# Prompt attention of a hybrid decoder: selected scores of unit n issued in turn with the sliding scores of unit n-1

## The reference

```python
p_c = masked_softmax(einsum('bqghd,bcgd->bqghc', qg, kc), mask_c)   # 63 compressed blocks
p_s = masked_softmax(einsum('bqghd,bqgmd->bqghm', qg, k_s), mask_s) # selected blocks, causal
p_w = masked_softmax(einsum('bqghd,bkgd->bqghk', qg, kw), mask_w)   # window of 512, causal
o = gt[..., 0:1] * o_c + gt[..., 1:2] * o_s + gt[..., 2:3] * o_w    # each o_x = p_x @ v_x
```

## Time and profile before

| | us |
|---|---|
| time, median of 2 runs | 3040.44 (3039.64 to 3041.25) |
| span of the profiled execution | 3041.8 |
| the four passes over the units, together | 472.50 |
| PE busy within them | 433.91 |

### The profile page before, as it was taken

One profiled execution on the slowest core, in us unless ns is written; L12 is line 12 of the kernel. 1 busy time (PEld: TensorE's weight loads), 2 busy tenths in 40 slices (PEclk: granted clock), 3 DMA queues, 4 the chain that ended last, 5 costly groups with the idle time before them and its releaser, 6 DMA issues. The chain is left out here.

```text
span 3041.8 us, 36642 instructions
## 1 busy us (share of the span) xinstructions
PE 2667.2 (88%) x12861; PEld 1881.7 (62%) x12861; DVE 1261.2 (41%) x2782; ACT 654.2 (22%) x1434; POOL 221.5 (7%) x197
## 2 busy tenths in 40 slices
PE   4989989898989877798989899599488889999999
PEld 2676867677676757465767666466255556666643
DVE  3456474756556465105453636345523330001012
ACT  2222121312222221003333334222032220000000
POOL 0012020101011020000000000022011100000000
PEclk8999999999999989897979697799688889999999
DMA  3101010110101000310000000354243314121001
GB/s 99 41 2 44 0 43 8 36 33 10 43 1 43 1 16 9 111 45 15 1 14 0 14 0 0 82 190 173 98 154 124 124 62 132 24 48 30 18 28 66
DMA packets 124355, 150.69 MB, mean 50 GB/s; under 512 B 30144, under 2 KB 107968, under 8 KB 115712
## 3 DMA queue, kind: packets, MB, share of 16 engines
q1 hardware_dynamic: 113152, 77.71, 9.4%
q0 software_dynamic: 11136, 72.17, 6.4%
HBM read 137.76 MB, written 16.26 MB: 51 GB/s over the span
## 5 line engine op out<-in xcount | busy, mean ns | idle before, releaser
L731 PE MATMUL g_ps<-hT,g_W 128*128 128x352 f32 x1536 | 487.4, 467 | 12.0 <-DMA g_W<-in_w_in_dram 12.0
L731 PEld LDWEIGHTS g_ps<-hT,g_W 128*128 128x128 f32 x1536 | 286.6, 194 | 151.1 <-issue 19.8
L2398 DVE SCALAR_TENSOR_TENSOR m_sg<-m_sg,m_ps 128x352 f32<-128x352 f32 x48 | 25.0, 521 | 360.6 <-PE m_ps L2338 360.6
L1369 PE MATMUL p_ps<-p_PTr,KV 128*128 128x128 f32 x1056 | 161.6, 305 | 1.9 <-ACT p_PTr L1428 1.9
L1369 PEld LDWEIGHTS p_ps<-p_PTr,KV 128*128 128x128 f32 x1056 | 143.4, 212 | 8.6 <-ACT p_PTr L1428 3.8
L1428 ACT COPY p_PTr<-p_ps 128x512 f32<-128x512 f32 (+3 forms) x176 | 86.2, 520 | 203.2 <-PE p_ps L1358 202.9
L2350 PE MATMUL m_ps<-m_Wo,m_mixed 128*128 128x512 f32 (+1 forms) x288 | 124.0, 593 | 1.4 <-DVE m_mixed L2401 1.4
L2331 PE MATMUL m_ps<-hT,Wgates 128*128 128x352 f32 x384 | 117.4, 465 | 1.5 <-DVEq L2387 1.5
L1389 PE MATMUL p_ps<-hT,Wpair 128*128 128x352 f32 x384 | 116.4, 466 | 1.2 <-SPq L1321 1.2
L1358 PE MATMUL p_ps<-identity,p_Pr 128*128 128x128 f32 x592 | 98.2, 302 | 20.2 <-DVEq L1501 20.0
L2331 PE MATMUL m_ps<-hT,m_Wgates 128*128 128x352 f32 x384 | 115.6, 459 | 0.0
(11 more groups left out here) (391 smaller groups left out, 4388.1 us busy)
## 6 DMA issues: line engine op xcount, KB each, us to landing
g_W<-in_w_in_dram SPq DMA_DIRECT2D x32, 512.0 KB, 5.2
n_x<-in_x_prompt_dram SPq DMA_DIRECT2D x8, 512.0 KB, 8.5
g_S<-in_state_gdn_dram SPq DMA_DIRECT2D x8, 512.0 KB, 7.0
out_dram<-g_S POOLq DMA_DIRECT2D x8, 512.0 KB, 3.9
Wpair<-in_w_in_dram SPq DMA_DIRECT2D x16, 256.0 KB, 4.4
Wgates<-in_w_in_dram SPq DMA_DIRECT2D x8, 512.0 KB, 5.2
m_Wgates<-in_w_in_dram SPq DMA_DIRECT2D x8, 512.0 KB, 4.8
m_Wo<-in_w_out_dram SPq DMA_DIRECT2D x1, 4096.0 KB, 16.2
```

The source lines that it names most:

```text
L731: ins = pe.matmul(ps[:, k.bank, 0:w], W[:, c_, kt, :], hT[:, kt, t0:t0 + w], start=kt == 0, stop=kt == KT - 1)
L1369: ins = pe.matmul(ps[:, k.bank, 0:P], v, PTr[0:r, u % 3, q, :], start=at + q == 0, stop=kind == "cmp")
```

## The change

Scores move into one function. In step n it waits for `slc_exp` of n-1 and `win_exp` of n-2, then issues the first slc part of unit n, the first win part of unit n-1, the second slc part, the second win part, and the cmp scores of n-1. Unit n and n-1 are of different groups, so the two use opposite 64 rows. Transposes and values follow for unit n-3, all in one piece. ACT's step is `exp_slc(n)`, the first two evacuations of n-3, `exp_win(n-1)`, the rest. DVE's step is the slc maximum of n, the win maxima of n-1, `weigh(n-2)`, `output(n-4)`. There are four `Pr` buffers for three, and three slots of `nmx` and `rs` for two. The loops run one step further.

```diff
-        Pr = [sb(f"Pr{n}", [P, CC + P]) for n in range(3)]
+        NPR = 4
+        Pr = [sb(f"Pr{n}", [P, CC + P]) for n in range(NPR)]
-        nmx = sb("nmx", [P, 2, 3])
-        rs = sb("rs", [P, 2, 3])
+        nmx = sb("nmx", [P, 3, 3])
+        rs = sb("rs", [P, 3, 3])
...
+                slc, win = [], []
+                if n < NU:
+                    pe.wait_ge(slc_exp, nth(i, n))
+                    slc = list(range(0, (units[n][0] + 1) * P, 512))
+                if 1 <= n <= NU:
+                    pe.wait_ge(win_exp, nth(i, n - 1))
+                    qt = units[n - 1][0]
+                    win = list(range(max(0, qt - 4) * P, (qt + 1) * P, 512))
+                for x in range(2):
+                    if x < len(slc):
+                        slc_part(slc[x])
+                    if x < len(win):
+                        win_part(win[x])
+                if win:
+                    cmp_part()
...
-                for n in range(NU + 2):
-                    if n < NU:
-                        scores_slc(i, n)
-                    if n >= 2:
-                        for u, _, ts in groups_of(units[n - 2][0])[:2]:
-                            turn(i, n - 2, u, ts)
-                    if n < NU:
-                        scores_win(i, n)
-                    if n >= 2:
-                        outputs(i, n - 2)
+                for n in range(NU + 3):
+                    scores(i, n)
+                    if n >= 3:
+                        for u, _, ts in groups_of(units[n - 3][0])[:2]:
+                            turn(i, n - 3, u, ts)
+                        outputs(i, n - 3)
...
-                for n in range(NU + 2):
-                    gs = groups_of(units[n - 2][0]) if n >= 2 else []
-                    for x in gs[:2]:
-                        evac(i, n - 2, *x)
-                    if n < NU:
-                        exp_slc(i, n)
-                    for x in gs[2:3]:
-                        evac(i, n - 2, *x)
-                    if n < NU:
-                        exp_win(i, n)
-                    for x in gs[3:]:
-                        evac(i, n - 2, *x)
+                for n in range(NU + 3):
+                    gs = groups_of(units[n - 3][0]) if n >= 3 else []
+                    if n < NU:
+                        exp_slc(i, n)
+                    for x in gs[:2]:
+                        evac(i, n - 3, *x)
+                    if 1 <= n <= NU:
+                        exp_win(i, n - 1)
+                    for x in gs[2:]:
+                        evac(i, n - 3, *x)
...
-                for n in range(NU + 3):
+                for n in range(NU + 4):
                     if n < NU:
-                        maxima(i, n, step)
+                        maxima_slc(i, n, step)
                     if 1 <= n <= NU:
-                        weigh(i, n - 1, step)
-                    if n >= 3:
-                        output(i, n - 3)
+                        maxima_win(i, n - 1, step)
+                    if 2 <= n <= NU + 1:
+                        weigh(i, n - 2, step)
+                    if n >= 4:
+                        output(i, n - 4)
```

More of the change, by code:

```diff
@@ L1327, in _, with scores, part, slc_part @@
         def _(pe):
[L1328 to L1334, removed]
+            def scores(i, n):
+                def part(n):
+                    qt, gr = units[n]
+                    rows = slice(gr * DN, (gr + 1) * DN)
+                    return qt, rows, qT[rows, qt * P:(qt + 1) * P]
+                def slc_part(k0):
+                    qt, rows, q = part(n)
@@ L1335, in scores_slc @@
                     w = min(512, (qt + 1) * P - k0)
                     ins = pe.matmul(s_slc[:, k0:k0 + w], q, g.slcT[rows, k0:k0 + w], start=True, stop=True)
[L1337 to L1345, removed]
+                    if k0 + w == (qt + 1) * P:
+                        ins.then_inc(slc_scores, 1)
@@ L1346, in scores_win, with win_part, cmp_part @@
+                def win_part(k0):
+                    qt, rows, q = part(n - 1)
+                    w0 = max(0, qt - 4) * P
                     w = min(512, (qt + 1) * P - k0)
                     pe.matmul(s_win[:, k0 - w0:k0 - w0 + w], q, g.winT[rows, k0:k0 + w], start=True, stop=True)
-                pe.matmul(s_win[:, 640:640 + NCB], q, g.kcT[rows, :], start=True, stop=True).then_inc(win_scores, 1)
+                def cmp_part():
+                    qt, rows, q = part(n - 1)
+                    pe.matmul(s_win[:, 640:640 + NCB], q, g.kcT[rows, :], start=True, stop=True).then_inc(win_scores, 1)
@@ L1357, in turn @@
                     c0 = {"slc": t * P, "win": WC + (t - max(0, qt - 4)) * P, "cmp": CC}[kind]
-                    ins = pe.transpose(ps[:, k.bank, q * P:(q + 1) * P], Pr[n % 3][:, c0:c0 + P], g.ident)
+                    ins = pe.transpose(ps[:, k.bank, q * P:(q + 1) * P], Pr[n % NPR][:, c0:c0 + P], g.ident)
                 ins.then_inc(a_filled, 1)
@@ L1410, in exp_slc @@
                 qt, gr = units[n]
-                w, m = (qt + 1) * P, n % 2
+                w, m = (qt + 1) * P, n % 3
                 act.wait_ge(slc_max, nth(i, n))
-                act.activation(Pr[n % 3][:, 0:w], s_slc[:, 0:w], ACT.Exp, bias=nmx[:, m, 0:1], accum_out=rs[:, m, 0:1]
+                act.activation(Pr[n % NPR][:, 0:w], s_slc[:, 0:w], ACT.Exp, bias=nmx[:, m, 0:1], accum_out=rs[:, m, 0:1]
                                ).then_inc(slc_exp, 1)
@@ L1417, in exp_win @@
                 qt, gr = units[n]
-                ww, m, out = (min(qt, 4) + 1) * P, n % 2, Pr[n % 3]
+                ww, m, out = (min(qt, 4) + 1) * P, n % 3, Pr[n % NPR]
                 act.wait_ge(win_max, nth(i, n))
@@ L1433, in _ @@
                     if x == "z":
-                        act.wait_ge(turn_done, i + 3)
+                        act.wait_ge(turn_done, i + NPR)
                     for s, (t0, w) in enumerate(THIRDS):
@@ L1459, in _, with maxima_slc @@
             v.wait_ge(c_loaded, 16)
-            for n in range(3):
+            for n in range(NPR):
                 v.memset(Pr[n][:, CC:CC + P], 0.0).then_inc(turn_done, 1)
-            def maxima(i, n, step):
+            def maxima_slc(i, n, step):
                 qt, gr = units[n]
-                m = n % 2
-                w, ww = (qt + 1) * P, (min(qt, 4) + 1) * P
+                m = n % 3
+                w = (qt + 1) * P
                 v.wait_ge(slc_scores, nth(i, n))
@@ L1469, in maxima, with maxima_win @@
                 v.tensor_reduce(nmx[:, m, 0:1], s_slc[:, 0:w], AX, ALU.max, negate=True).then_inc(slc_max, 1)
+            def maxima_win(i, n, step):
+                qt, gr = units[n]
+                m, ww = n % 3, (min(qt, 4) + 1) * P
                 v.wait_ge(win_scores, nth(i, n))
@@ L1485, in weigh @@
                 qt, gr = units[n]
-                m, pr = n % 2, Pr[n % 3]
+                m, pr = n % 3, Pr[n % NPR]
                 w, ww = (qt + 1) * P, (min(qt, 4) + 1) * P
```

## The result

The changed kernel takes 3063.91 us (median of two runs, 3058.96 and 3068.87) against 3040.44: a ratio of 1.007 (95% interval 1.0054 to 1.0087). It is a little slower, by less than 2%. Four later runs of the same kernel gave 3057.74 (3057.35 to 3061.16), ratio 1.0052 (1.0036 to 1.0067).

The account below looks back on a forecast made before the run. PE's own work was taken to set the step in the middle of a pass. -0.6 - 5.6 + 5.8 = -0.4 us a pass; 3041.8 - 1.6 + 9.6 (clock) gave 3050, own range 3020 to 3080.

Parts of the forecast that it names:

- the likeliest case: Whole kernel: forecast 3050 us, own range 3020 to 3080, chance 0.66.
- Overlap: Slc and win scores on opposite halves fully overlap; PE alone would be 12.6 us shorter in steps 8 to 15.
- The new wait: Values wait for copies behind exp_slc(n) on ACT; steps 8 to 14 come to 49.4 us against 50.00.
- First stretch: Steps 0 to 7 of a pass: 42.0 us against 47.60, a gain of 5.6 us.
- Drain: Step 15 and three draining steps of a pass: 25.9 us against 20.10, 5.8 us lost.
- Clock: PE's new gaps lower the clock: two falls a pass at 1.2 us each, 9.6 us in four passes.
- The rule on PSUM evacuation: Tiling speeds up TensorE but not evacuation, which may then bind; the saving doesn't come and time stays where it was.
- PE still sets the step: Rival: PE's work counts, about 20 us less a pass, 2960, halfway 3000; chance 0.12 with halfway cases.
- The halves don't overlap: Rival: slc's second part waits for a win matmul, 12 us a pass more, 3098; chance 0.12.
- The gaps cost the clock: Rival: lower clock in most steps from 8 on, 12 to 43 us a pass, 3090 to 3210; chance 0.10.

Follow-up runs that it names:

- on one half: Changed kernel with win and cmp scores of unit n-1 computed from unit n's 64 rows, so no overlap: 3113.64 us, ratio 1.0229.
- the reordered kernel: Changed kernel with the first two evacuations ahead of exp_slc(n) and the third ahead of exp_win(n-1): 2981.43 us, ratio 0.9802; second chip 2979.45.
- the kernel with the wait filled: Changed kernel plus 8 to 18 unread identity transposes in PE's wait in each of steps 8 to 15: 3045.72 us, ratio 1.0008.
- The reordered kernels: Changed kernel with two evacuations ahead of exp_slc(n): 3007.06 us; with the third also ahead of exp_win(n-1): 2981.43 us.

## Why the prediction was right, and where its terms were off

Direction and mechanism hold, and the time lies within the likeliest case's own range; the point was 8 to 14 us too low, and that it came so close is in part luck: two errors of opposite sign nearly cancelled. By its steps:

- *Overlap.* Taken as full, and it is: a win part costs 0.86 us on one half and nothing beside slc on the other. PE's busy time of the middle fell by 6.4 us (48.26 to 41.84), though that includes three stretches in which matmuls ran at half speed. In the reordered kernel, without such stretches, it is 38.61: 9.7 less in seven steps, where 12.6 in eight had been worked out. Starts within 0.02 us, which the prediction named as the sign, were not seen for the 512-column passes of step 14: they start some 0.2 us apart and interleave.
- *The new wait.* Values idle 1.24 to 2.34 us in steps 8 to 15 of pair 1, released by ACT's copy; 1.5 to 2.5 was said. The chain's sum for steps 8 to 14, 49.4 us, is for the full clock, and at the full clock it measures 50.2 (the kernel with the wait filled). Sums from rows of the old trace were good to 2%.
- *First stretch.* 38.6 us instead of 42.0. The lower clock lasted 27.3 us, until 31 us into the pass, where the sum put all steps up to 7 at that price; in the kernel before it lasted 41.0 us, and on one half 41.0 again. How much of the further gain is the overlap's own and how much comes from the earlier rise of the clock was not taken apart.
- *Drain.* 28.0 instead of 25.9. Step 15 was put at 8.8 and measures 8.8 with the wait filled, 10.4 with the fall; the step after it takes 6.6 rather than 6.1, the two last 5.5 each as said.
- *Clock.* This term was mis-sized. Two falls a pass at 1.2 us were taken; four came. The three in the middle cost 4.8 us together (55.0 less 50.2), the one in step 15 1.6, so 6.4 us a pass and not 2.4. Over four passes that is 16 us more than the forecast had.
- *Together.* Taking pair 1 for each of the four passes: +16 for the falls, +3.2 for the chain (0.8 a pass), +2 for the drain (0.5 a pass), -13.6 for the first stretch (3.4 a pass), 7.6 us above the forecast. The four passes measure 486.60 against 480.5 forecast (472.50 - 1.6 + 9.6), 6.1 above. The two-run median lies 14 us above the forecast, the four later runs 8. The two errors that nearly cancelled are the falls (+16) and the first stretch (-13.6).

The rule on PSUM evacuation that the prediction weighed (the Trainium skill, TensorEngine Tiling (Array Packing), Performance Considerations, PSUM Bottleneck) gives the outcome of the change as it stands: the saving did not come, and the wait is for the copies. The reordered kernels show that this was not the evacuation's capacity. With the same number of copies on the same engine the wait falls from 84.2 to 20.9 us when they stand ahead of the exps.

The rivals: *PE still sets the step* had its condition (under 0.5 us of wait a step) unmet at 1.3 us a unit; it is what happens in the reordered kernel, at 0.33 us and 2980 us, near the 2960 worked out for it. *The halves don't overlap* was priced at 48 us more and measured 50 to 56 when made true; it is not what happened. *The gaps cost the clock* was right in kind, with a granted clock of 0.91 rather than below 0.8.

Open: which wait drops the clock. In pair 1 falls followed waits of 1.86, 2.21, 2.34 and 2.33 us, but none followed waits of 1.73, 1.68 and 2.10. Busy time by stretch, as around the wait of 2.34 us above: here the wait of 2.10 us lies in the first row, and the dense work behind it, still at 1.00, in the second.

```profile
1606.00:1609.60 3.60, 1.52 (x15) 1.17 (x11) 2.88 (x7) 1.61 (x4) 0.00 (x0) 1.00 0.00 0
1609.70:1613.00 3.30, 3.30 (x29) 3.18 (x31) 2.28 (x9) 1.93 (x5) 0.00 (x0) 1.00 0.00 0
```

The length of the wait alone does not sort the cases (1.86 us did it, 2.10 did not), and no run tested what does. In the reordered kernels, where the values wait for 1.1 us at most, no fall came from step 8 on.

## What to carry to other kernels

When two matmul streams are packed side by side, look at once for the first thing behind them in the lists of the engines that drain PSUM: an operation that waits for the newest scores must not stand ahead of copies of older results, since PE then waits for copies that could have been made earlier. Here the packed scores were worth 72 us, and the place of the evacuations in ACT's list decided whether the kernel became 0.5 to 0.7% slower or some 2% faster. Price a new wait on PE twice: for its own length, and for the stretch at the lower clock that dense work behind it may run into (1.6 us here for a wait of some 2 us).

## What the runs showed of the hardware

- Matmuls on opposite 64 rows start out of their order in the program. `slc_part` is issued as a whole ahead of `win_part`, yet in the timeline of step 14 win's first pass (1612.76) starts before slc's first (1613.08), and win's second (1613.30) before slc's second (1613.51). The Trainium skill, TensorE: Matmul & The Clock Gate, Part 3, has matmuls in program order in start and end; the recorded starts differ from that for f32 passes on different rows.
- Two streams of 512 columns in f32, on 64 rows each, run at full rate: slc passes 0.43 us apart with or without win beside them.
- The clock fell after waits of about 2 us with dense work behind them; the earlier trace rows had shown a fall only in a stretch of 3.50 us without a matmul.
- With 112 more transposes in a pass, PE idled 2.6 to 3.0 us with "issue" as the cause ahead of each next pass (8.3 us in three), and the queue of instructions moved 60 packets instead of 32. That the loading of the longer loop is the cause is likely but not shown.
